# Queries, keys and values split and turned in the combine stage, with scores as stacked bf16 products

## What is computed

```python
def swa_sink_attention(hn, w_q, w_o, sinks, k, v, cos, sin):
    q = apply_rope((hn @ w_q).reshape(B, S, N_Q_HEADS, HEAD_DIM), cos, sin)
    q = (q * (HEAD_DIM ** -0.5)).reshape(B, nb, BLOCK, N_KV_HEADS, Q_PER_KV, HEAD_DIM)
    kb = banded_blocks(k, nb)
    vb = banded_blocks(v, nb)
    s = jnp.einsum('bnqkgd,bnjkd->bnkgqj', q, kb).astype(jnp.float32)
    ...
    pr = (e / (jnp.sum(e, axis=-1, keepdims=True) + jnp.exp(sink - m))).astype(vb.dtype)
    o = jnp.einsum('bnkgqj,bnjkd->bnqkgd', pr, vb).reshape(B, S, N_Q_HEADS * HEAD_DIM)
    return o @ w_o
```

## Time and profile before

| | us |
|---|---|
| Median of 3 runs | 5042.87 |
| Lowest and highest | 5032.93, 5050.52 |
| Profiled execution, its own time | 5047.73 |
| Span of the profile | 5046.1 |
| Combine, some 1585 to 2492 | 907 |
| Attention, from 2492 | some 830 |

### The profile page before, as it was taken

How to read it: one execution, slowest core, us unless ns; L and a number is a source line. 1 busy time by engine, 2 the same in 40 slices (tenths; PEclk the granted TensorE clock), 3 DMA queues, 4 the chain that set the end, 5 groups by cost and what they waited for, 6 DMA issues and landing times. The chain is left out here.

```text
span 5046.1 us, 92066 instructions
## 1 busy us (share of the span) xinstructions
PE 4639.1 (92%) x29091; PEld 2960.2 (59%) x29513; DVE 2871.9 (57%) x5911; ACT 2021.1 (40%) x2962; POOL 1607.1 (32%) x1163
## 2 busy tenths in 40 slices
PE   7986999999995899999789999986999999997999
PEld 6954677676664344444356666643776767665444
DVE  5775444444444555555488888874444444443666
ACT  5844443344332222222155555544343344331343
POOL 1103443444340111111033333313444444431332
PEclk9987999999998999999899999998999999998999
DMA  7968898888885666666477777757888889885664
GB/s 234 320 231 286 267 307 286 274 297 263 277 282 173 187 187 192 189 183 185 111 173 178 178 179 178 176 174 256 287 285 278 290 271 300 267 270 168 241 231 168
DMA packets 1153018, 1170.87 MB, mean 232 GB/s; under 512 B 824480, under 2 KB 852128, under 8 KB 1152928
## 3 DMA queue, kind: packets, MB, share of 16 engines
q1 hardware_dynamic: 1106848, 1035.48, 69.0%
q0 software_dynamic: 46080, 134.27, 7.8%
HBM read 738.57 MB, written 270.53 MB: 200 GB/s over the span
## 5 line engine op out<-in xcount | busy, mean ns | idle before, releaser
L837 POOL TENSOR_TENSOR ex_w_lo<-ex_raw,ex_w_hi 128x2048 bf16<-128x2048 f32 x192 | 780.0, 4086 | 1105.3 <-ACT ex_w_hi L896 1105.3
L896 ACT ACTIVATE ex_w_hi<-ex_raw 128x2048 bf16<-128x2048 f32 x384 | 707.1, 1900 | 385.8 <-PE ex_ps_y L112 189.5
L1008 PE MATMUL ex_ps_gate<-ex_xT,ex_w_hi 128*128 128x0 bf16 x2048 | 568.0, 278 | 135.5 <-DMA ex_xT<-ex_xrow 97.3
L1009 PE MATMUL ex_ps_gate<-ex_xT,ex_w_hi 128*128 128x0 bf16 x2048 | 567.8, 277 | 0.0
L1010 PE MATMUL ex_ps_gate<-ex_xT,ex_w_lo 128*128 128x0 bf16 x2048 | 567.7, 277 | 0.0
L1008 PE MATMUL ex_ps_up<-ex_xT,ex_w_hi 128*128 128x0 bf16 x2048 | 558.8, 273 | 0.0
L1009 PE MATMUL ex_ps_up<-ex_xT,ex_w_hi 128*128 128x0 bf16 x2048 | 558.6, 273 | 0.0
L1010 PE MATMUL ex_ps_up<-ex_xT,ex_w_lo 128*128 128x0 bf16 x2048 | 558.4, 273 | 0.0
L988 DVE COPY ex_y<-ex_ps_y 128x512 f32 x324 | 223.9, 691 | 566.8 <-PE ex_ps_y L112 564.4
L972 DVE TENSOR_TENSOR ex_aT<-ex_silu,ex_ps_up 128x384 bf16<-128x384 f32 x256 | 141.7, 553 | 681.2 <-PE ex_ps_up L1010 501.4
L111 PE MATMUL ex_ps_y<-ex_w_lo,ex_aT 128*128 128x512 bf16 x1296 | 492.1, 380 | 8.5
(11 more groups left out here) (353 smaller groups left out, 9571.7 us busy)
## 6 DMA issues: line engine op xcount, KB each, us to landing
ex_raw<-in_w_exp_gate SPq DMA_DIRECT2D x128, 1024.0 KB
ex_raw<-in_w_exp_up SPq DMA_DIRECT2D x128, 1024.0 KB, 11.5
ex_raw<-in_w_exp_down SPq DMA_DIRECT2D x128, 1024.0 KB, 5.8
y_rows<-ex_y SPq DMA_DIRECT2D x162, 512.0 KB, 2.9
up_rows<-rt_up_out SPq DMA_DIRECT2D x64, 512.0 KB, 2.6
cb_hin<-h_mid SPq DMA_DIRECT2D x64, 512.0 KB, 4.1
cb_up_in<-up_rows SPq DMA_DIRECT2D x64, 512.0 KB, 4.7
mix_x<-in_x SPq DMA_DIRECT2D x32, 512.0 KB, 5.3
```

The lines of the kernel that those rows point to most:

```text
L837: eng.tensor_tensor(w_lo[u][:, w], raw[:, c, :], w_hi[u][:, w], ALU.subtract).then_inc(lo_done, 1)
L896: act.activation(w_hi[u][:, c * WCHUNK:(c + 1) * WCHUNK], raw[:, c, :], ACT.Copy).then_inc(hi_done, 1)
L1008: pe.matmul(out, hi, x_hi, start=j == 0, stop=False)
L1009: pe.matmul(out, hi, x_lo, start=False, stop=False)
```

## The change

In combine, queries, keys and values are split into bf16 high and low parts right after the rotation: ScalarE writes the high parts (three copies), VectorE the low parts (three subtractions). A query head becomes a row of 128 (64 high, 64 low); a key head becomes two rows of 128, high twice and low twice. Two DMA transposes (16 blocks for the queries, 8 for the keys) turn them, and three stores write them out as `qT_rows` (512 KB a tile), `kT_rows` (256 KB) and `v_rows` (128 KB). The transposes are issued at the end of a step, the stores in the next step behind x3's transpose. The squares of the two norms are written into `x` and `x3` in place of `junk`, and the query rows reuse the weights' landing buffers `raw`.

In attention the ten transposes, the copies out of PSUM and the split of the values go. Queries and keys are loaded turned; the keys and values have a ring of four buffers, and the loop is unrolled by four tiles in place of two. The scores of a pair are eight bf16 products of K = 128 and 128 columns: for each of two heads and two key blocks, the stacked query by the high key and by the low key.

```diff
@@ combine, VectorE, tail
-                    wait(dve, q_st, 32 * t)
...
-                    rotate(t, at, ps_kv[:, 0:KVW], kv_out[:, 0:KVW], NKV, 2, kv_mm, t + 1, False)
-                    dve.tensor_copy(kv_out[:, KVW:2 * KVW], ps_kv[:, KVW:2 * KVW]).then_inc(v_done, 1)
+                    rotate(t, at, ps_kv[:, 0:KVW], k_out[:], NKV, 2, kv_mm, t + 1, False)
+                    dve.wait_ge(qh_done, t + 1)
+                    dve.tensor_tensor(q_row[:, :, 1, :], q_out[:].rearrange("p (n e) -> p n e", e=HEAD), q_row[:, :, 0, :],
+                                      ALU.subtract).then_inc(ql_done, 1)
+                    dve.wait_ge(vh_done, t + 1)
+                    dve.tensor_tensor(v_row[:, 1, :], ps_kv[:, KVW:2 * KVW], v_row[:, 0, :], ALU.subtract).then_inc(vl_done, 1)
+                    dve.wait_ge(kh_done, t + 1)
+                    dve.wait_ge(rot_add, 3 * t + 3)
+                    dve.tensor_tensor(k_row[:, :, 1, :, :], k_out[:].rearrange("p (j e) -> p j e", e=HEAD).unsqueeze(2).to_broadcast([P, NKV, 2, HEAD]),
+                                      k_row[:, :, 0, :, :], ALU.subtract).then_inc(kl_done, 1)
@@ combine, SP: step, at its start and at its end
                     turn(x3T, x3, x3_turned)
+                    if not (isinstance(t, int) and t == 0):
+                        store_qkv(t - 1)
...
-                    sp.wait_ge(rot_add, 3 * t + 3)
-                    sp.dma_start(q_t[t], q_out[:]).then_inc(q_st, 16)
-                    sp.wait_ge(v_done, t + 1)
+                    sp.wait_ge(ql_done, t + 1)
                     sp.sem_inc(turn_open, 1)
-                    sp.dma_start(kv_t[t], kv_out[:]).then_inc(q_st, 16)
+                    sp.wait_ge(kl_done, t + 1)
+                    sp.sem_inc(turn_open, 1)
+                    wait(sp, qkv_st, 48 * t)
+                    sp.sem_inc(turn_open, 1)
+                    sp.dma_start(q_turned.rearrange("p (n m) -> p n m", m=P), q_row.rearrange("p n two e -> p (n two e)"),
+                                 transpose=True).then_inc(qk_turned, 16)
+                    sp.dma_start(k_turned[:], k_row[:].rearrange("p j a b e -> p (j a b e)"),
+                                 transpose=True).then_inc(qk_turned, 16)
@@ combine, SP: the stores
+            def store_qkv(t):
+                sp.wait_ge(qk_turned, 32 * t + 32)
+                sp.sem_inc(turn_open, 1)
+                at = slice(t, t + 1) if isinstance(t, int) else bass.ds(t, 1)
+                for rows, src in ((C.qT_rows, q_turned), (C.kT_rows, k_turned[:].rearrange("p j n -> p (j n)")),
+                                  (C.v_rows, v_row[:].rearrange("p h n -> p (h n)"))):
+                    sp.dma_start(rows[at].rearrange("o p n -> (o p) n"), src).then_inc(qkv_st, 16)
@@ attention, SP: loads
-                if load:
-                    wait(sp, turn_mm, s + 1)
-                    sp.dma_start(q_in[u][:], q_t[s + 2]).then_inc(q_ld[u], 16)
...
-                    if c == 5 and load:
-                        wait(sp, v_done, s + 1)
-                        sp.dma_start(kv_in[u][:], kv_t[s + 2]).then_inc(kv_ld[u], 16)
+                    if c == 5 and load and cur:
+                        sp.wait_ge(s_mm, pairs(s, NP - 1))
+                        sp.sem_inc(turn_open, 1)
+                        load_q(s + 2, u)
+                        wait(sp, pv_mm, 2 * s)
+                        sp.sem_inc(turn_open, 1)
+                        load_kv(s + 2, (r + 2) % KR)
@@ attention, TensorE: scores
-                for b, keys in ((0, kT[1 - par]), (1, kT[par])):
-                    mm = pe.matmul(ps_s[:, c % 2, :, b * P:(b + 1) * P], qT[par][:, c, :], keys[:, jj, :, :],
-                                   start=True, stop=True)
+                for k in (0, 1):
+                    for b, keys in ((0, kT[(r - 1) % KR]), (1, kT[r])):
+                        for part in (0, 1):
+                            mm = pe.matmul(ps_s[:, c % 2, k, b * P:(b + 1) * P], qT[r % 2][:, 2 * c + k, :],
+                                           keys[:, 2 * jj + k, part, :], start=part == 0, stop=part == 1)
                 mm.then_inc(s_mm, 1)
```

More of the change, by code:

```diff
@@ L1881, in _ @@
         def _(pool):
-            for u in (0, 1):
-                pool.memset(kT[u][:], 0.0).then_inc(fixed, 1)
-                pool.memset(vp[u][:], 0.0).then_inc(fixed, 1)
+            pool.memset(kT[KR - 1][:], 0.0).then_inc(fixed, 1)
+            pool.memset(vp[KR - 1][:], 0.0).then_inc(fixed, 1)
             def heads(t, c):
@@ L1934, in step @@
                         exps(s + 1, c + 3 - NP)
-                    if c == 1 and nxt:
-                        act.wait_ge(turn_mm, s + 2)
-                        wait(act, s_mm, NP * s)
-                        act.activation(qT[v][:], ps_t[:], ACT.Copy).then_inc(qT_done, 1)
                     if c == 1 and prev2:
@@ L1946, in step @@
                         out_hi(s - 1, 1)
-                    if c == 2 and cur:
-                        act.wait_ge(kv_ld[u], done(s, u))
-                        wait(act, pv_mm, 2 * s)
-                        act.wait_ge(fixed, 4)
-                        vin = kv_in[u][:, KVW:2 * KVW].rearrange("p (j e) -> p j e", e=HEAD)
-                        act.activation(vp[u][:, 0, :, :], vin, ACT.Copy).then_inc(vh_done, 1)
                     if c == 3 and prev2:
@@ L2043, in step @@
                         out_lo(s - 1, 1)
-                    if c == 4 and nxt:
-                        dve.wait_ge(turn_mm, s + 2)
-                        wait(dve, s_mm, NP * (s + 1))
-                        dve.wait_ge(fixed, 4)
-                        for k in (0, 1):
-                            rows = slice(HEAD * k, HEAD * k + HEAD)
-                            last = dve.tensor_copy(kT[v][rows, :, k, :], ps_k[rows, :, :])
-                        last.then_inc(kT_done, 1)
-                        if isinstance(s, int) and s == -1:
-                            sinks()
-                    if c == 4 and cur:
-                        dve.wait_ge(vh_done, s + 1)
-                        vin = kv_in[u][:, KVW:2 * KVW].rearrange("p (j e) -> p j e", e=HEAD)
-                        dve.tensor_tensor(vp[u][:, 1, :, :], vin, vp[u][:, 0, :, :], ALU.subtract).then_inc(v_done, 1)
+                    if c == 4 and isinstance(s, int) and s == -1:
+                        sinks()
                     if c == 3 and prev2:
@@ L2112, in project, with step @@
                 return mm
-            def step(s, u, load, nxt, cur, prev, prev2):
+            def step(s, r, load, nxt, cur, prev, prev2):
+                u = r % 2
                 v = 1 - u
@@ L2130, in step @@
                         project(1, 0)
-                    if c == 1 and nxt:
-                        t = s + 1
-                        pe.wait_ge(q_ld[v], done(t, v))
-                        pe.wait_ge(kv_ld[v], done(t, v))
-                        wait(pe, log_done, s - 2)
-                        wait(pe, ol_done, 2 * s - 1)
-                        for k in range(KD):
-                            pe.transpose(ps_t[:, k * P:(k + 1) * P], q_in[v][:, k * P:(k + 1) * P], C.ident[:])
-                        for j in (0, 1):
-                            mm = pe.transpose(ps_k[:, j, :], kv_in[v][:, j * P:(j + 1) * P], C.ident[:])
-                        mm.then_inc(turn_mm, 1)
                     if c == 2 and prev:
-                        weigh(s - 1, v, 1)
+                        weigh(s - 1, (r - 1) % KR, 1)
                     if c == 3 and prev2:
                         pe.wait_ge(hn_done, s - 1)
-                        if nxt:
-                            pe.wait_ge(qT_done, s + 2)
-                        else:
-                            wait(pe, log_done, s - 2)
+                        wait(pe, log_done, s - 2)
                         for k in range(KD):
```

129 lines of the change are left out of this document (76 added, 53 removed).

## The result

The changed kernel is slower: 5107.22 us (median of 4 runs, 5093.78 to 5112.9) against 5041.98 for the kernel before (4 runs, 5032.93 to 5050.52), a ratio of 1.0126 with a 95% interval of [1.0099, 1.0152]. The forecast of 4999 and the whole of its range were too low. The profiled execution took 5107.4 us, its span is 5105.7.

A forecast was written before the change was run, and what follows sets the result against it. TensorE was taken to bound combine and attention, with VectorE next in attention. Attention -116 us and combine +72 us sum to -44 us: 5047.7 profiled becomes 5004, median 4999 us, range 4937 to 5060.

The forecast's parts named there:

- the block price of a transpose: Combine, SP queue: a DMA transpose costs 0.15 us a block and 1.9 us fixed, so 40 blocks take 7.9 us.
- Forecast +72: Combine: 60 us of stalls over 30 tiles, 4 us at the last tile, 8 us at the stage's end.
- (1): Combine: transposes run at the 401 GB/s of plain copies, so no stall comes; combine costs only 10 us, 4937; chance 0.12.
- Rival (3): Combine: the three transposes run one after another, 11.7 us, a stall of 5.8 us a tile, 5113; chance 0.10.
- the sum of TensorE's work: Attention: TensorE saves 5.3 us a tile on scores and turning and would need 18.9 us.
- the chain of 21.6 us: Attention: hand-overs between TensorE, ScalarE and VectorE through one tile sum to 21.6 us, taken as 21.5.
- the piece that I put at 9.35 us: Attention: from VectorE's first-half subtraction through 24 products, two pairs, weighing, ScalarE's copy and VectorE's subtraction, 9.35 us.
- the two others: Attention, rest of the tile: 0.3, 24 products 5.2, one pair and pick-up 0.6 us; then VectorE without a gap, 6.2 us.
- a low clock: Attention: a low granted clock from TensorE's new gaps, named as what would make the forecast wrong; no size or chance given.
- tile of 21.5 us: Attention: forecast time a tile, a gain of 3.6 us, 108 us over 30 tiles; bounds 20.6 and 23.
- the forecast's lower bound: Attention: VectorE's own work of 20.5 us a tile, more than TensorE's 18.9.
- Rival (2): Attention: the DMA engines fill, weights' transposes come late, a tile takes 23.3 us, 5053 in all; chance 0.18.

The follow-up runs named there:

- the kernel with filling: Changed kernel with x3's transpose issued first, VectorE's attention loop of two tiles, and 9 and 3 unread TensorE products a tile ahead of its oT waits: 4959.76 us.
- the earlier hand-over: Changed kernel, x3's transpose first, VectorE's loop of two tiles, ScalarE copying oT before its exponentials, VectorE subtracting the first half at the start of c = 7: 4936.33 us.
- the hand-over alone: Changed kernel with only ScalarE's oT copies put ahead of the exponentials and VectorE's first-half subtraction at the start of c = 7: 5032.9 us.
- both fills: Changed kernel with unread TensorE products ahead of its oT waits, nine at c = 0 and three at c = 4: 5060.3 us.
- the earlier subtraction: Changed kernel with VectorE's subtraction of the first half of oT put ahead of one pair's score operation at c = 7: 5089.3 us.

## Why the prediction was wrong

- **Combine, right and a little small.** The stall per tile was forecast at 2.0 us, from the block price of a transpose; it is 1.98 on average. The forecast's order and release are the ones in the trace. Forecast +72, measured +83. The 30 waits make 59.4 us (forecast 60), and the last tile's 11.9 us is 4.4 more than the 7.5 that it had before (forecast 4). Two things were not in the sum: the first tile's wait is 9.8 instead of 6.5 us, and behind 5 of the 30 waits the clock falls (periods near 30 us instead of 28, as from SP's 1800.91 to 1831.02), some 8 us if each costs 1.7 as in attention, which is an estimate. Rivals (1) and (3), 0 and 5.8 us of stall, are out. Rival (3) had a whole time of 5113, near the measured 5107; that is luck, since it put a miss into combine that happened in attention.
- **Attention, the sum of TensorE's work, right.** Sixteen score products take 0.99 us (2909.20 to 2910.19), 0.062 each where the step had 0.055.
- **Attention, the chain of 21.6 us, wrong in one link.** The step "ScalarE's copy and VectorE's subtraction with their pick-up 1.5" left out that ScalarE makes two exponentials (2 x 0.5) before the copy. In the kernel with filling the piece that I put at 9.35 us is 2911.51 - 2901.54 = 9.97, the two others are 6.1 and 6.2 as forecast, sum 22.3. The rows of the kernel before had the right price: from the end of the weighing (2704.16 + 1.49) to the end of the subtraction (2707.20 + 0.69) pass 2.24 us, not 1.5. With the earlier hand-over the tile goes from 22.36 to 21.44 us, attention by 764.6 - 735.2 = 29 us; that is more than the 0.6 of this link, and the edit moves the other half's copy and subtraction too; the two shares were not measured apart.
- **Attention, the clock: the step that failed.** The forecast expected TensorE "waiting for oT some 2 us" and two sentences later named a low clock as what would prove it wrong, but gave it no price and no chance; its tile of 21.5 us holds all products at the price that they have at a granted clock of 1.00. (The low clock of its stage start is a granted clock of 0.50 from 2492 to 2504 us in the kernel before.) In the changed kernel's tiles every wait for oT of 2.0 to 2.5 us has some 3 us at a granted clock of 0.50 behind it, 1.7 us lost; filling gave back 810.8 - 764.6 = 46 us.
- **Attention, the loop: not in the forecast at all.** The diff lengthens the loop from two to four tiles on every engine. I read this as bookkeeping for the ring of four. It costs 19 us.
- The three make 29 + 46 + 19 = 94 us, of 92 that were missing. They were measured in kernels with different rests, so their sum is good to a few us. The kernel with the hand-over alone checks it: 74.4 us, where the hand-over without the clock and the clock make 29 + 46 = 75.
- **The 21.5 us, reached by another road.** That the mended kernel has 21.44 us a tile is in part luck. The forecast had it as a chain over three engines; in the mended kernel that chain is shorter, and VectorE is busy 98% of the tile, some 21 us. Its share of the sum was right: in the changed kernel it is busy 166.61 / 200 x 24.64 = 20.5 us a tile, the forecast's lower bound.
- **Rival (2)** had attention gain little because the DMA engines fill. The gain was that small, but no TensorE wait for a DMA stands in attention's list of waits from 2700 to 3300 us, and at 21.44 us a tile, with a DMA share of 0.86 to 0.89, the only one from 2650 to 3180 us is of 0.7 us.

With order, loop and hand-over mended the changed kernel takes 4936.33 us, and the kernel before with the same hand-over 5018.8 us (one run), so the turned, stacked scores are worth some 82 us. In attention that is 821.7 - 735.2 = 86.5 us and not the forecast's 116: the other 30 are the hand-over's, which the kernel before can have as well. Unmended, order, loop and hand-over cost 5107.2 - 4936.3 = 171 us, more than the scores give.

## What to carry over

In this kernel's attention a wait of 2.0 to 2.5 us that the change put onto TensorE cost its length and then 1.7 us at a granted clock of 0.50; in combine the clock fell at 5 of 30 such waits. Price a wait with the clock behind it in mind, and look first whether the hand-over behind it can be made earlier by changing the order on the two engines that serve it (75 us here). Put new transfers into a queue behind the one that the busiest engine waits for, not ahead of it (82 us here). And when a ring of buffers makes a loop longer, look at every engine where its loop goes round, and leave the loop short on an engine that stalls there and doesn't need the ring, as VectorE here (19 us).

## What the runs showed of the hardware

- In attention the granted clock fell to 0.50 at single TensorE waits for oT of 1.6 to 2.5 us, once or twice a tile. It held behind waits of 0.65 (changed kernel), 0.87 (kernel before), 1.28 (hand-over alone) and 1.49 us (both fills). The length of a wait doesn't decide it alone: in combine 25 of 30 waits of 1.7 to 2.4 us passed without a fall, and in attention three in a row with the earlier subtraction (1.84, 1.91 and 2.36 us, from 2754 to 2791 us) and two waits of 2.4 and 2.5 us for another pair of scores (2781.64, 3139.19) with the hand-over alone. What else decides was not measured.
- VectorE stood still 3.5 to 4.0 us a round in the changed kernel, where its loop holds four tiles of this stage (4.3 at most with the hand-over alone, 2.8 in the kernel before with such a loop), and not at all with two; in the changed kernel ScalarE, GpSimd and TensorE's products went round four tiles without such rows from 2650 to 3340 us.
- TensorE took 9 + 3 unread products a tile and the stage became faster, 764.6 us instead of 810.8, because they stood in its waits and the granted clock was 1.00 from 2700 to 2900 us instead of 0.93.
